# Order of the small float32 matmuls in a hybrid decoder's mixer: by array half instead of in turn

## The chip, the cores and the metric

The kernel runs on one core of one Trainium2 chip. The metric is the device time of one launch in microseconds. Before the change it is 1982.39 us, the median of three runs (1982.12 to 1985.22).

TensorE (PE in the profile) multiplies: a stationary operand (the weights, up to 128 rows by 128 columns) is loaded, a moving operand streams past it, and the result is written or added into PSUM, eight banks of 128 partitions by 512 float32. VectorE (DVE), ScalarE (ACT) and GpSimd (POOL) do the rest; SyncE (SP) issues most DMAs. A matmul whose operands have 64 rows uses the upper or the lower half of the array's rows, by the partitions on which they lie; one whose stationary operand has 64 columns uses the left or the right half of its columns, by the partitions to which it writes.

## The reference, cut to what matters

Two layers, each of them a SwiGLU half, a mixer and a second SwiGLU half, over 512 prompt tokens and 32 sample tokens (8 sequences of 4). The mixer has a sliding-window attention (8 query heads, 2 key/value heads of 64 dimensions, window 128, learned sinks) and a gated linear attention (GLA, 4 heads, key 64, value 128, chunks of 64 tokens):

```python
qg = q.reshape(B, N, Q, SWA_KV_HEADS, SWA_GROUP, HEAD_DIM)
s = jnp.einsum('bnqhgd,bnkhd->bnhgqk', qg, k) * (HEAD_DIM ** -0.5)
...
o = jnp.einsum('bnhgqk,bnkhd->bnqhgd', probs.astype(v.dtype), v)
```
```python
def step(S, inp):
    ...
    att = jnp.where(causal, jnp.einsum('bhid,bhjd->bhij', qb, kc * jnp.exp(-b)), 0.0)
    o = jnp.einsum('bhij,bhjv->bhiv', att, vc) + jnp.einsum('bhid,bhdv->bhiv', qb, S)
    S = jnp.exp(b_last[..., 0, :])[..., None] * S + jnp.einsum('bhjd,bhjv->bhdv', kc * jnp.exp(b_last - b), vc)
    return S, o
```

## The kernel before, in words

All activations stay in SBUF, feature-major: 8 tiles of 128 features by 544 tokens. The big products (projections and SwiGLU) take each weight as a high and a low part in fp32r and use three matmuls for each product (`product`, L769; `unit_product`, L809). They hold most of TensorE's time. The small products of the mixer are plain float32 and are what the change touches.

The order of each engine's work in a mixer is written out by hand: `mixer_steps()` makes one list `STEPS` that all engines walk through, and each engine does its share of every step. Steps named `in` are projection tiles; the small steps stand between them, so that VectorE and ScalarE work on one small step while TensorE does the next projection. Each engine's program is a fixed sequence, and it waits on semaphores.

The steps with small matmuls on TensorE that matter here:

- `score` (L1013), eight a layer, one for each pair of query block `b` (4) and head pair group `jj` (2). It computes four score tiles: `uu` is the head in the pair, `g` the key/value head. `g` picks partitions 0 to 63 or 64 to 127 of `qS` and `kS`, so the half of the array's rows, and writes to bank 4 + g. Block 0 has one key block (128 columns), the others have two (256 columns).
- `pv` (L1040), eight a layer: probabilities times values. `g` picks which 64 partitions of bank 6 are written, so the half of the array's columns; `kb` runs over one or two key blocks that are added up.
- `samp_s` (L1051, L1055), once a layer: scores of the sample tokens against the cache, for 8 sequences `b` and two row halves `g`, added up in PSUM over `b`.
- `kv` (L1126), eight steps a layer in four pairs: the state update of a GLA chunk. The chunk's half picks the rows, the head `hh` picks the columns, so there are four different quarters. An odd step does nothing here; the even one does both chunks and signals `kv_done` by 2.
- `att` (L1141) and `o` (L1155, L1163), four a layer: `o` adds, per head, one full matmul (values by masked scores, 128 rows) and for each of the two chunks a matmul of the state with the queries (64 rows, half picked by `hh`). In `o` 0 only one chunk has a state. The next step is `kv` or a projection.

`L975`, `L1185`, `L1191`, `L1203`, `L1216` and `L1229` are small products that the change leaves alone. VectorE's softmax of a unit starts with `score_done` (L2069), its copies of attention results with `pv_done` (L2178), the state update with `kv_done` (L2225, L2230), ScalarE's copy of the GLA output with `o_done` (L1635).

Of the kernel before, what the change touches and what calls it, by code (L numbers as in the profile page):

```python
# [24 lines left out]
P = 128  # L25
# [3 lines left out]
NB = 8  # L29
# [7 lines left out]
WIN = 128  # L37
HD = 64
PAST = 2048
EPS = 1e-6  # L40
CHUNK = 64
# [162 lines left out]
def trunk(nc, xT, stream, gains, lparams, wa2, cos_t, sin_t, swa_mask, samp_mask, gla_mask,  # L204
# [14 lines left out]
    with ctx:  # L219
# [18 lines left out]
        s_ring = sb("s_ring", [P, 4, 2, P], at=big)  # L238
# [38 lines left out]
        qG = mx("qG", [P, 2, T], 2 * U)  # L277
# [9 lines left out]
        kc = mx("kc", [P, NB, WIN], 13 * U)  # L287
        qz = mx("qz", [P, NB * (P + 16)], 15 * U)
# [473 lines left out]
        def _(pe):  # L762
# [183 lines left out]

            def product_order(b):

                return [(kb, g) for kb in range(0 if b else 1, 2) for g in range(2)]

            def mixer(l):
                ch = l * PL_LAYER + PL_MIX
                stage = l * 3 + 1
                for pos, (step, i) in enumerate(STEPS):
# [48 lines left out]
                    elif step == "score":  # L1003
# [5 lines left out]
                        o = 0 if b else WIN  # L1009
                        for uu in range(2):  # L1010
                            for g in range(2):
                                rows = slice(g * HD, (g + 1) * HD)
                                ins = pe.matmul(ps[:, 4 + g, uu * 256 + o:(uu + 1) * 256],  # L1013
                                                qS[rows, 2 * jj + uu, b * WIN:(b + 1) * WIN],
                                                kS[rows, k0:(b + 1) * WIN], start=True, stop=True)
# [18 lines left out]
                    elif step == "pv":  # L1034
                        b, jj = UNITS[i]
                        pe.wait_ge(m["pt_out"], i + 1)
                        for uu in range(2):
                            for kb, g in product_order(b):
                                o = (2 * g + uu) * 256 + kb * WIN
                                ins = pe.matmul(ps[g * HD:(g + 1) * HD, 6, uu * WIN:(uu + 1) * WIN],  # L1040
                                                vs_tok[:, b - 1 + kb, g * HD:(g + 1) * HD], p_t[:, o:o + WIN],
                                                start=kb == (0 if b else 1), stop=kb == 1, skip_group_check=True)
                        ins.then_inc(m["pv_done"], 1)
                    elif step == "samp_s":
                        pe.wait_ge(m["loaded"], 16 * N_LOADS)
                        pe.wait_ge(m["masked"], len(UNITS))
                        pe.wait_ge(m["q_set"], 1)
                        for b in range(NB):
                            for g in range(2):
                                rows = slice(g * HD, (g + 1) * HD)  # L1050
                                pe.matmul(ps[:, 4 + g, 0:WIN], qz[rows, b * P:(b + 1) * P], kc[rows, b, :],  # L1051
                                          start=b == 0, stop=b == NB - 1, skip_group_check=True)
                        for g in range(2):
                            rows = slice(g * HD, (g + 1) * HD)
                            ins = pe.matmul(ps[:, 4 + g, WIN:WIN + SAMP], qc[rows, :],  # L1055
                                            kS[rows, SEQ:T], start=True, stop=True)
# [60 lines left out]
                    elif step == "kv":  # L1117

                        if i % 2:
                            continue  # L1120
                        pe.wait_ge(m["att_out"], i // 2 + 1)
                        for h in range(GH):
                            pr, hh = divmod(h, 2)
                            for c in range(2):
                                rows = slice(c * CHUNK, (c + 1) * CHUNK)
                                ins = pe.matmul(ps[hh * HD:(hh + 1) * HD, 4 + c, pr * P:(pr + 1) * P],  # L1126
                                                klT[rows, i // 2, h * HD:(h + 1) * HD],
                                                v_tok[rows, i // 2, h * P:(h + 1) * P], start=True, stop=True)
                        ins.then_inc(m["kv_done"], 2)
                    elif step == "att":  # L1130
# [13 lines left out]
                    elif step == "o":  # L1144
# [8 lines left out]
                        for h in range(GH):  # L1153
                            pr, hh = divmod(h, 2)
                            pe.matmul(ps[:, 6 + hh, pr * P:(pr + 1) * P], v_tok[:, i, h * P:(h + 1) * P],  # L1155
                                      attm[:, i % 2, hh, pr, :], start=pr == 0, stop=False, skip_group_check=True)
                        for c in (2 * i, 2 * i + 1):
                            if c == 0:
                                continue
                            for pr in range(2):  # L1160
                                for hh in range(2):
                                    o = pr * P + (c % 2) * CHUNK
                                    ins = pe.matmul(ps[:, 6 + hh, o:o + CHUNK],  # L1163
                                                    s_ring[hh * HD:(hh + 1) * HD, c % 4, pr, :],
                                                    qG[hh * HD:(hh + 1) * HD, pr, c * CHUNK:(c + 1) * CHUNK],
                                                    start=False, stop=c == 2 * i + 1, skip_group_check=True)
                        ins.then_inc(m["o_done"], 1)
# [1306 lines left out]
```

## Time and profile before

| | us |
|---|---|
| median of 3 runs | 1982.39 |
| profiled execution, its own time | 1982.39 |
| span, first to last instruction | 1980.6 |
| TensorE busy | 1929.6 (97%) |
| VectorE busy | 1352.1 (68%) |
| ScalarE busy | 1103.3 (56%) |
| GpSimd busy | 1094.7 (55%) |

The two mixers lie at about 400 to 600 us and 1370 to 1575 us of the span. TensorE records come in two kinds: PE is the matmul, PEld the load of its stationary operand, which may overlap other matmuls. Matmuls overlap in their records, since the end of one is modelled with its way through the array, so what one costs in a stream is better read from the start of one group to the start of the next than from its duration. One float32 matmul of the program gives two PE records and two PEld records. In the forms, `64*128` is the stationary operand's rows and columns, and `64x256` the moving operand's partitions and columns.

### The profile page before, as it was taken

The numbers are of one execution on the slowest core, as the hardware profiler recorded it, in microseconds if no ns is written. First come the engines' busy times: TensorE is split into PE (matmuls) and PEld (weight loads), VectorE is DVE, ScalarE is ACT, GpSimd is POOL, SyncE is SP. The second block draws the span as 40 slices with busy tenths as digits, with TensorE's granted clock in tenths as the row PEclk, the third lists the DMA queues.
The fourth block names the chain that finished last, engine by engine and source line by source line (L and its number), as shares of the span: only waits on it lengthen the run. The fifth ranks groups of instructions, "written<-read, shape, count | busy, mean of one in ns | idle before, by whom it ended". The sixth has DMA issues, their size and how long they took to land.

```text
span 1980.6 us, 40845 instructions
## 1 busy us (share of the span) xinstructions
PE 1929.6 (97%) x15562; PEld 1899.0 (96%) x15562; DVE 1352.1 (68%) x2450; ACT 1103.3 (56%) x2184; POOL 1094.7 (55%) x811
## 2 busy tenths in 40 slices
PE   5999999999999999999999999999999999999997
PEld 5999999998989999999999999999888899999997
DVE  7976687487345986578678757865774458756774
ACT  4664566536234665566656646663552366645662
POOL 3675566732215566566766656675222166655663
PEclk9999999999989999999999999999998999999998
DMA  4233232421212233232323333224221222332331
GB/s 138 84 108 106 89 101 92 141 86 54 99 57 75 76 110 96 95 105 95 99 81 102 102 102 101 98 94 133 75 98 45 68 80 94 101 107 91 102 110 59
DMA packets 92114, 185.65 MB, mean 94 GB/s; under 512 B 12880, under 2 KB 22768, under 8 KB 91376
## 3 DMA queue, kind: packets, MB, share of 16 engines
q1 hardware_dynamic: 84096, 170.04, 26.2%
q10 hardware_dynamic: 7824, 13.00, 1.9%
q8 instruction: 124, 2.03, 0.4%
q14 instruction: 70, 0.57, 0.1%
HBM read 178.09 MB, written 6.95 MB: 93 GB/s over the span
## 4 chain that ended last, share of the span: by engine, by line
PE 90%; DVE 8%; issue 1%; ACT 1%; DMA 0%; POOLq 0%; POOL 0%; DVEq 0%; ACTq 0%
PE ps L809 56%; PE ps L769 21%; PE ps L818 7%; PE ps L1216 1%; PE ps L797 1%; PE ps L1229 1%; PE ps L1030 0%; PE ps L1040 0%; DVE t L2195 0%; DVE st L2074 0%; PE ps L1191 0%; DVE qS L2289 0%; PE ps L1013 0%; DVE h_end L1711 0%; PE ps L789 0%
## 5 line engine op out<-in xcount | busy, mean ns | idle before, releaser
L809 PE MATMUL ps<-rhs,w_hi 128*128 128x272 f32 x4256 | 805.0, 289 | 0.0
L809 PEld LDWEIGHTS ps<-rhs,w_hi 128*128 128x128 f32 x4256 | 669.7, 188 | 0.7 <-DVE ssum L1898 0.7
L809 PE MATMUL ps<-rhs,w_lo 128*128 128x272 f32 x2128 | 614.1, 289 | 0.0
L646 POOL TENSOR_TENSOR w_lo<-w_raw,w_hi 128x512 fp32r<-128x512 f32 x272 | 351.3, 1297 | 251.6 <-ACT w_hi L1316 251.6
L640 POOL TENSOR_TENSOR w_lo<-w_raw,w_hi 128x1024 fp32r<-128x1024 f32 x80 | 192.0, 2402 | 385.8 <-ACT w_hi L1260 371.1
L809 PEld LDWEIGHTS ps<-rhs,w_lo 128*128 128x128 f32 x2128 | 402.4, 189 | 0.0
L809 PE MATMUL ps<-act_c,w_hi 128*128 128x272 f32 x1792 | 354.5, 289 | 1.1 <-DVE h_mid L1749 0.8
L646 POOL TENSOR_TENSOR w_lo<-s_tmp,w_hi 128x512 fp32r<-128x512 f32 x216 | 282.9, 1321 | 32.9 <-ACT w_hi L1316 32.6
L809 PEld LDWEIGHTS ps<-act_c,w_hi 128*128 128x128 f32 x1792 | 287.7, 188 | 1.8 <-DVE h_mid L1749 1.2
L769 PE MATMUL ps<-h_mid,w_hi 128*128 128x272 f32 x1600 | 279.2, 293 | 0.0
L809 PE MATMUL ps<-act_c,w_lo 128*128 128x272 f32 x896 | 258.3, 288 | 0.0
L769 PEld LDWEIGHTS ps<-h_mid,w_hi 128*128 128x128 f32 x1600 | 230.0, 191 | 3.4 <-issue 2.8
L1316 ACT ACTIVATE w_hi<-ps 128x512 fp32r<-128x512 f32 x216 | 129.2, 598 | 182.1 <-DVE ps L1774 171.1
L1316 ACT ACTIVATE w_hi<-w_raw 128x512 fp32r<-128x512 f32 x272 | 172.0, 632 | 47.5 <-PE ps L809 40.3
L1316 ACT ACTIVATE w_hi<-s_tmp 128x512 fp32r<-128x512 f32 x216 | 136.7, 633 | 87.3 <-PE ps L809 85.9
L809 PEld LDWEIGHTS ps<-act_c,w_lo 128*128 128x128 f32 x896 | 169.3, 189 | 0.0
L769 PE MATMUL ps<-h_mid,w_lo 128*128 128x272 f32 x800 | 166.5, 290 | 0.0
L1774 DVE TENSOR_TENSOR s_tmp<-ps,w_raw 128x512 f32<-128x512 f32 x216 | 148.4, 687 | 17.2 <-POOL w_lo L646 3.1
L818 PE MATMUL ps<-act_p,pl_hi 128*128 128x272 f32 x768 | 159.4, 287 | 0.0
L1260 ACT ACTIVATE w_hi<-w_raw 128x1024 fp32r<-128x1024 f32 x76 | 80.1, 1057 | 129.9 <-PE ps L769 118.6
L1774 DVE TENSOR_TENSOR ps<-ps,w_raw 128x512 f32<-128x512 f32 x216 | 149.6, 692 | 2.8 <-ACT ps L1367 0.7
L1780 DVE TENSOR_TENSOR w_lo<-ps,w_hi 128x512 fp32r<-128x512 f32 x216 | 141.4, 684 | 1.2
(292 smaller groups left out, 3215.8 us busy)
## 6 DMA issues: line engine op xcount, KB each, us to landing
w_raw<-stream SPq DMA_DIRECT2D x380, 256.0 KB, 2.9
w_raw<-stream SPq DMA_DIRECT2D x80, 512.0 KB, 3.3
g_buf<-stream SPq DMA_DIRECT2D x52, 256.0 KB, 2.8
pl_raw<-stream SPq DMA_DIRECT2D x64, 192.0 KB, 2.8
x<-xT ACTq DMA_DIRECT2D x8, 272.0 KB, 5.9
y_d<-x SPq DMA_DIRECT2D x8, 272.0 KB, 2.1
s<-s_d ACTq DMA_DIRECT2D x2, 1024.0 KB, 5.3
s_s_d<-s ACTq DMA_DIRECT2D x2, 1024.0 KB, 3.9
```

What stands on the lines that cost most here:

```text
L640: pool.tensor_tensor(w_lo[:, p % RING, :], w_raw[:, p % RAW, :], w_hi[:, p % RING, :].bitcast(F32), ALU.subtract).then_inc(lo_ready, 1)
L646: pool.tensor_tensor(operand(w_lo, j, half), source(op, s, half), operand(w_hi, j, half).bitcast(F32), ALU.subtract).then_inc(pool_low, 1)
L769: ins = pe.matmul(dst[:, hf, :], w[:, slot, cols], r[:, hf * TH:(hf + 1) * TH], start=first and w is w_hi and r is rhs_hi, stop=last and r ...
L797: ins = pe.matmul(ps[:, 6 + at // TH, o:o + w], nrt[0:w, c:c + 1].to_broadcast([w, P]), ident[0:w, 0:w], start=True, stop=True)
L809: ins = pe.matmul(bank(s, at), w[:, k * P:(k + 1) * P], moving[:, k, side, r, :], start=fresh and k == 0 and w is hi and side == 0, stop=k ...
L818: ins = pe.matmul(bank(s, at), w[:, k * P:(k + 1) * P], act_p[:, k, side, hf * TH:(hf + 1) * TH], start=False, stop=k == PLAIN - 1 and sid ...
L1216: ins = pe.matmul(ps[0:w, 4, c:c + 1], sq_tile(h)[:, tb * P:tb * P + w], ones[:, 0:1], start=True, stop=True)
L1229: ins = pe.matmul(ps[:, 4 + 2 * (i % 2) + tb // 4, (tb % 4) * P:(tb % 4) * P + w], rt[0:w, c:c + 1].to_broadcast([w, P]), ident[0:w, 0:w], ...
L1260: act.activation(w_hi[:, p % RING, :], w_raw[:, p % RAW, :], ACT.Copy).then_inc(hi_ready, 1)
L1316: act.activation(operand(w_hi, j, half), source(op, s, half), ACT.Copy).then_inc(op_high, 1)
L1774: dve.tensor_tensor(source(name, s, half), first, second, ALU.add).then_inc(sum_made, 1)
L1780: dve.tensor_tensor(operand(w_lo, j, half), source(op, s, half), operand(w_hi, j, half).bitcast(F32), ALU.subtract).then_inc(dve_low, 1)
```

## The change

Five steps of TensorE's program are written in another order. The matmuls and their operands are the same.

- `score`: both `uu` of g = 0 first, then both of g = 1 (before: g = 0, g = 1 in turn).
- `pv`: all of g = 0, then all of g = 1 (before: in turn), by `a` from 0 to 3.
- `samp_s`: all eight sequences and the new tokens of g = 0, then of g = 1.
- `kv`: every step does its own chunk, with its own wait and its own signal of 1; before, the even step did both chunks in turn.
- `o`: head by head: the full matmul of a head, then its one or two state matmuls, then the next head. `start` is now set for each head, before only for the first of a bank.

```diff
-                        for uu in range(2):
-                            for g in range(2):
-                                rows = slice(g * HD, (g + 1) * HD)
+                        for g in range(2):
+
+                            rows = slice(g * HD, (g + 1) * HD)
+                            for uu in range(2):
                                 ins = pe.matmul(ps[:, 4 + g, uu * 256 + o:(uu + 1) * 256],
...
-                        for uu in range(2):
-                            for kb, g in product_order(b):
-                                o = (2 * g + uu) * 256 + kb * WIN
+                        for a in range(4):
+                            g, uu = divmod(a, 2)
+                            for kb in range(0 if b else 1, 2):
+                                o = a * 256 + kb * WIN
                                 ins = pe.matmul(ps[g * HD:(g + 1) * HD, 6, uu * WIN:(uu + 1) * WIN],
                                                 vs_tok[:, b - 1 + kb, g * HD:(g + 1) * HD], p_t[:, o:o + WIN],
...
-                        for b in range(NB):
-                            for g in range(2):
-                                rows = slice(g * HD, (g + 1) * HD)
-                                pe.matmul(ps[:, 4 + g, 0:WIN], qz[rows, b * P:(b + 1) * P], kc[rows, b, :],
-                                          start=b == 0, stop=b == NB - 1, skip_group_check=True)
                         for g in range(2):
                             rows = slice(g * HD, (g + 1) * HD)
+                            for b in range(NB):
+                                pe.matmul(ps[:, 4 + g, 0:WIN], qz[rows, b * P:(b + 1) * P], kc[rows, b, :],
+                                          start=b == 0, stop=b == NB - 1)
...
-                        if i % 2:
-                            continue
                         pe.wait_ge(m["att_out"], i // 2 + 1)
+                        rows = slice((i % 2) * CHUNK, (i % 2 + 1) * CHUNK)
                         for h in range(GH):
                             pr, hh = divmod(h, 2)
-                            for c in range(2):
-                                rows = slice(c * CHUNK, (c + 1) * CHUNK)
-                                ins = pe.matmul(ps[hh * HD:(hh + 1) * HD, 4 + c, pr * P:(pr + 1) * P],
...
-                        ins.then_inc(m["kv_done"], 2)
+                            ins = pe.matmul(ps[hh * HD:(hh + 1) * HD, 4 + i % 2, pr * P:(pr + 1) * P],
...
+                        ins.then_inc(m["kv_done"], 1)
...
                         for h in range(GH):
                             pr, hh = divmod(h, 2)
-                            pe.matmul(ps[:, 6 + hh, pr * P:(pr + 1) * P], v_tok[:, i, h * P:(h + 1) * P],
-                                      attm[:, i % 2, hh, pr, :], start=pr == 0, stop=False, skip_group_check=True)
-                        for c in (2 * i, 2 * i + 1):
-                            if c == 0:
-                                continue
-                            for pr in range(2):
-                                for hh in range(2):
-                                    o = pr * P + (c % 2) * CHUNK
+                            at, bank = pr * P, 6 + hh
+                            pe.matmul(ps[:, bank, at:at + P], v_tok[:, i, h * P:(h + 1) * P],
+                                      attm[:, i % 2, hh, pr, :], start=True, stop=False)
+                            for c in (2 * i, 2 * i + 1):
+                                if c == 0:
+                                    continue
+                                o = at + (c % 2) * CHUNK
```

TensorE's program around the second `o` of a layer (step `o` 1, after `att` 2 and before `kv` 4), before the change. L1155 and L1163 are the full matmuls and the state matmuls; in the changed file they are L1149 and L1155:

```order
L1141 MATMUL ps<-qG,kG 128x128 x4
L1155 MATMUL ps<-attm,v_tok 128x128 x4
L1163 MATMUL ps<-qG,s_ring 128x64 x8
L1126 MATMUL ps<-v_tok,klT 64x128 x8
L943 MATMUL ps<-g_buf,ones 128x272 x2
```

and of the changed kernel:

```order
L1134 MATMUL ps<-qG,kG 128x128 x4
L1149 MATMUL ps<-attm,v_tok 128x128
L1155 MATMUL ps<-qG,s_ring 128x64 x2
L1149 MATMUL ps<-attm,v_tok 128x128
L1155 MATMUL ps<-qG,s_ring 128x64 x2
L1149 MATMUL ps<-attm,v_tok 128x128
L1155 MATMUL ps<-qG,s_ring 128x64 x2
L1149 MATMUL ps<-attm,v_tok 128x128
L1155 MATMUL ps<-qG,s_ring 128x64 x2
L1119 MATMUL ps<-v_tok,klT 64x128 x8
```

The four full matmuls, which stood together, now stand each ahead of its own head's two state matmuls.

TensorE's program at the first pair of `kv` steps, with the waits, before:

```order
L1141 MATMUL ps<-qG,kG 128x128 [waits m_ga_out]
L1141 MATMUL ps<-qG,kG 128x128 x3
L1126 MATMUL ps<-v_tok,klT 64x128 [waits m_att_out]
L1126 MATMUL ps<-v_tok,klT 64x128 x7
L769 MATMUL ps<-h_mid,w_hi 128x272 [waits lo_ready,m_in_used]
```

and of the changed kernel:

```order
L1134 MATMUL ps<-qG,kG 128x128 [waits m_ga_out]
L1134 MATMUL ps<-qG,kG 128x128 x3
L1119 MATMUL ps<-v_tok,klT 64x128 [waits m_att_out]
L1119 MATMUL ps<-v_tok,klT 64x128 x3
L1119 MATMUL ps<-v_tok,klT 64x128 [waits m_att_out]
L1119 MATMUL ps<-v_tok,klT 64x128 x3
L769 MATMUL ps<-h_mid,w_hi 128x272 [waits lo_ready,m_in_used]
```

The eight matmuls are split in two groups of four, one for each row half, with a wait ahead of each. In `score`, `pv` and `samp_s` the rows of the program look the same before and after, since the matmuls of both halves have the same names and shapes; what moves there is what the diff shows.

## Rows read from the trace of the kernel before

**Rows 1.** The profile's page, sections 1 and 4.
```profile
PE 1929.6 (97%) x15562; PEld 1899.0 (96%) x15562; DVE 1352.1 (68%) x2450; ACT 1103.3 (56%) x2184; POOL 1094.7 (55%) x811
...
PE 90%; DVE 8%; issue 1%; ACT 1%; DMA 0%; POOLq 0%; POOL 0%; DVEq 0%; ACTq 0%
```

**Rows 2.** Waits of TensorE, 410 to 610 us: waited for, us, times, longest.
```profile
PE ps L769 <- DVE mixS_lo L2093: 2.4, 2, 1.6
...
PE ps L1030 <- DVE qS L2178: 1.1, 2, 0.8
...
PE ps L1110 <- DVE vG L2132: 0.5, 1, 0.5
```

**Rows 3.** Busy time by window, L1013 alone: window, length, busy (xinstructions), clock, DMA.
```profile
433.39:433.45 0.06, 0.05 (x2) 0.05 (x2) 1.00 0.00 0
433.45:433.71 0.26, 0.26 (x2) 0.25 (x4) 1.00 0.00 0
```

**Rows 4.** Timeline, two narrow windows: start, us, engine, line, op, tiles, count.
```profile
433.73 0.59 PE L1013 MATMUL ps<-kS,qS 64*128 64x256 f32 x3
...
434.15 0.38 PE L1013 MATMUL ps<-kS,qS 64*128 64x256 f32 x2
```

**Rows 5.** Busy time by window, L975 alone, then L1203 alone.
```profile
444.90:445.10 0.20, 0.19 (x1) 0.19 (x2) 1.00 0.00 0
...
552.30:552.37 0.07, 0.06 (x8) 0.07 (x10) 1.00 0.63 234
```

**Rows 6.** Timeline of TensorE, pv, score and the transposes after them, 432.8 us.
```profile
432.81 0.66 PE L1040 MATMUL ps<-a_buf,vs_tok 128*64 128x128 f32 x8
433.40 1.14 PE L1013 MATMUL ps<-kS,qS 64*128 64x256 f32 x8
434.46 1.09 PE L1030 MATMUL ps<-ident,sq_buf 128*128 128x128 f32 x8
```

**Rows 7.** Timeline of TensorE, a later pv and short score, and samp_s.
```profile
452.23 1.09 PE L1040 MATMUL ps<-a_buf,vs_tok 128*64 128x128 f32 x16
453.25 0.72 PE L1013 MATMUL ps<-kS,qS 64*128 64x128 f32 x8
453.94 1.06 PE L1030 MATMUL ps<-ident,sq_buf 128*128 128x128 f32 x8
...
494.74 2.06 PE L1051 MATMUL ps<-kc,qz 64*128 64x128 f32 x32
496.63 0.31 PE L1055 MATMUL ps<-kS,qc 64*128 64x32 f32 x4
```

**Rows 8.** Timeline of TensorE, steps o and kv.
```profile
539.80 0.66 PE L1163 MATMUL ps<-qG,s_ring 64*128 64x64 f32 x8
540.39 0.67 PE L1126 MATMUL ps<-v_tok,klT 64*64 64x128 f32 x16
...
547.84 1.16 PE L1155 MATMUL ps<-attm,v_tok 128*128 128x128 f32 x8
548.93 1.11 PE L1163 MATMUL ps<-qG,s_ring 64*128 64x64 f32 x16
549.97 0.67 PE L1126 MATMUL ps<-v_tok,klT 64*64 64x128 f32 x16
550.56 1.18 PE L943 MATMUL ps<-g_buf,ones 128*128 128x272 f32 x4
...
568.60 1.05 PE L1155 MATMUL ps<-attm,v_tok 128*128 128x128 f32 x8
569.58 1.11 PE L1163 MATMUL ps<-qG,s_ring 64*128 64x64 f32 x16
```

**Rows 9.** Busy time by window, all engines, and the granted clock (PEclk).
```profile
530.40:533.70 3.30, 3.30 (x15) 3.30 (x16) 1.03 (x3) 0.00 (x0) 0.58 (x1) 0.50 0.02 5
547.00:552.00 5.00, 4.75 (x55) 3.61 (x53) 2.67 (x7) 2.96 (x4) 2.35 (x1) 1.00 0.04 8
578.40:588.20 9.80, 9.80 (x47) 9.74 (x47) 0.31 (x3) 0.41 (x2) 0.00 (x0) 0.50 0.45 174
```

More of the change, by code:

```diff
@@ L945, in square_sum @@
                 return ins
-            def product_order(b):
-                return [(kb, g) for kb in range(0 if b else 1, 2) for g in range(2)]
             def mixer(l):
@@ L1036, in mixer @@
                         pe.wait_ge(m["pt_out"], i + 1)
-                        for uu in range(2):
-                            for kb, g in product_order(b):
-                                o = (2 * g + uu) * 256 + kb * WIN
+                        for a in range(4):
+                            g, uu = divmod(a, 2)
+                            for kb in range(0 if b else 1, 2):
+                                o = a * 256 + kb * WIN
                                 ins = pe.matmul(ps[g * HD:(g + 1) * HD, 6, uu * WIN:(uu + 1) * WIN],
                                                 vs_tok[:, b - 1 + kb, g * HD:(g + 1) * HD], p_t[:, o:o + WIN],
-                                                start=kb == (0 if b else 1), stop=kb == 1, skip_group_check=True)
+                                                start=kb == (0 if b else 1), stop=kb == 1)
                         ins.then_inc(m["pv_done"], 1)
@@ L1117, in mixer @@
                     elif step == "kv":
-                        if i % 2:
-                            continue
                         pe.wait_ge(m["att_out"], i // 2 + 1)
+                        rows = slice((i % 2) * CHUNK, (i % 2 + 1) * CHUNK)
                         for h in range(GH):
                             pr, hh = divmod(h, 2)
-                            for c in range(2):
-                                rows = slice(c * CHUNK, (c + 1) * CHUNK)
-                                ins = pe.matmul(ps[hh * HD:(hh + 1) * HD, 4 + c, pr * P:(pr + 1) * P],
-                                                klT[rows, i // 2, h * HD:(h + 1) * HD],
-                                                v_tok[rows, i // 2, h * P:(h + 1) * P], start=True, stop=True)
-                        ins.then_inc(m["kv_done"], 2)
+                            ins = pe.matmul(ps[hh * HD:(hh + 1) * HD, 4 + i % 2, pr * P:(pr + 1) * P],
+                                            klT[rows, i // 2, h * HD:(h + 1) * HD],
+                                            v_tok[rows, i // 2, h * P:(h + 1) * P], start=True, stop=True)
+                        ins.then_inc(m["kv_done"], 1)
                     elif step == "att":
@@ L1154, in mixer @@
                             pr, hh = divmod(h, 2)
-                            pe.matmul(ps[:, 6 + hh, pr * P:(pr + 1) * P], v_tok[:, i, h * P:(h + 1) * P],
-                                      attm[:, i % 2, hh, pr, :], start=pr == 0, stop=False, skip_group_check=True)
-                        for c in (2 * i, 2 * i + 1):
-                            if c == 0:
-                                continue
-                            for pr in range(2):
-                                for hh in range(2):
-                                    o = pr * P + (c % 2) * CHUNK
[L1163 to L1166, printed above, removed]
+                            at, bank = pr * P, 6 + hh
[5 more added lines that the diff above has]
+                                o = at + (c % 2) * CHUNK
+                                ins = pe.matmul(ps[:, bank, o:o + CHUNK],
+                                                s_ring[hh * HD:(hh + 1) * HD, c % 4, pr, :],
+                                                qG[hh * HD:(hh + 1) * HD, pr, c * CHUNK:(c + 1) * CHUNK],
+                                                start=False, stop=c == 2 * i + 1)
                         ins.then_inc(m["o_done"], 1)
```

## The prediction, made before the changed kernel ran

> **What bounds the kernel now.** I read the page first. TensorE is busy for 1929.6 of 1980.6 us, and it has 90% of the chain that ended last [rows 1]. So a microsecond added to TensorE's own work costs a microsecond, unless TensorE would otherwise wait there for somebody. The waits are few: between 410 and 610 us, one layer's mixer, TensorE waits 2.4 us for DVE's mixS_lo, 1.1 us for its qS and 0.5 us for its vG [rows 2]. The second layer's mixer is built alike. The edit touches five steps of the mixer on TensorE, twice (two layers): eight `score`, eight `pv`, one `samp_s`, four pairs of `kv`, four `o` per layer. No operand, shape or DMA changes; only the order of the matmuls, and `kv` has two waits and two signals where it had one.
>
> **What small matmuls do side by side.** These are float32 matmuls, and each shows as two records: four score matmuls are x8, sixteen of L1203 x32. I call a record a pass. In narrow windows one sees how many run at once: L1013 (64 rows, g = 0 and g = 1 in turn) has 2 in its first 60 ns, and up to 433.71 still 2, with 4 weight loads: the two next passes have their weights and wait [rows 3]. They start at 433.73, 0.33 after the first two, and from there to the last two at 434.15 two rounds take 0.42, 0.21 each [rows 4]. L975, both matmuls on the same 16 rows, has 1; L1203, which goes over eight different places of the array, has 8 in its first 60 ns [rows 5]. So passes on different parts of the array (row halves, column halves, quarters) run together, passes on the same part one after another, and the blocked second pass of one matmul does not hold back the first pass of the next matmul on another part. The order before always puts different parts next to each other; the order after puts all work of one half first. The question is how far the array looks past a blocked pass.
>
> The Trainium skill, TensorE: Matmul & The Clock Gate, Part 3, says that only weight loads are pulled ahead when the row group differs, and that matmuls start and end in program order. The trace disagrees: by that rule the second pass of a matmul would stand in front of the next matmul, and there could not be 8 under way within 60 ns. With that rule the order before would already be nearly serial, and the sum below would shrink to its `o` term.
>
> **What the rows of before give as unit costs.** I measure a group from its start to the start of the next group.
> - Full score (256 columns): 433.40 to 434.46, 1.06 us for 4 rounds of two passes [rows 6]; the first round is 0.10 longer than the others [rows 4], which I read as a first weight load that nothing hides. Short score (128 columns): 0.69 us [rows 7].
> - pv: 0.59 us for 4 rounds [rows 6], 1.02 for 8 [rows 7]: 0.43 for 4 more, 0.109 a round.
> - samp_s: 1.89 us for 16 rounds [rows 7], at most 0.118 a round; I take the 0.112 of L1163 below, which has the same weights.
> - kv: four passes at once, 0.59 us for 4 rounds [rows 8].
> - o: L1155, 128 rows, 8 passes one after another, 1.09 us when it comes from 64-row matmuls (547.84) and 0.98 when it comes from 128-row ones (568.60); L1163, 64 rows, 0.59 us for 4 rounds, 1.04 for 8, so 0.112 a round [rows 8]. What stands over the rounds (0.59 - 3 x 0.112 = 0.25 instead of 0.11) is the price of coming from and going to another split of the array.
>
> **o, step by step.** After the edit each head does its one 128-row matmul, then its one or two 64-row matmuls on one half, then the next head's 128-row one: eight changes of split where there were two, and the 64-row passes no longer have a partner, whatever the array looks past, since the 128-row matmul between needs all of it. Per head with two chunks: 128-row part 1.09 - 6 x 0.112 = 0.42, 64-row part 4 passes alone = the 4 rounds' 0.59; 1.01. Four heads 4.04 against 1.09 + 1.04 = 2.13: +1.9 us, three times a layer. In o 0 only one chunk: 0.42 + 0.59 - 2 x 0.112 = 0.79, four times 3.15, against 1.09 + 0.59 = 1.68: +1.5 us. Per layer 7.2 us. The low end: were the changes of split free once they repeat, 6 passes of 0.112 per head are 2.7 against 2.13, so +0.6, and +0.1 for o 0: 1.8 per layer.
>
> **score, pv, samp_s, kv.** No row shows a queue of several blocked passes on one part. From below the cost is 0 (the array finds the other half's work however far back). Below nothing it cannot go: no pass is dropped, and two halves are all there is. From above it is fully serial: score +0.85 and +0.45 (4 rounds), pv +0.87 and +0.44, samp_s +1.8, kv +1.3 a pair; 19 us a layer. I take the value nearest to rows 3: a part holds one running pass and one waiting with its weights loaded, and the third one blocks everything behind it. Then the second half starts when the first half's last but one pass is done, with its first weight load in the open (0.10 us; 0.05 for pv's 64 columns):
> - full score: 2 rounds later, 2 x 0.213 + 0.10 = 0.53, six times; short 2 x 0.112 + 0.10 = 0.32, twice: 3.8
> - pv: 8 passes a half, 6 x 0.109 + 0.05 = 0.70, six times; block 0 with 4 passes 0.27, twice: 4.7
> - samp_s: 16 passes a half, 14 x 0.112 + 0.10 = 1.7
> - kv: column halves still alternate, row halves do not: 2 x 0.109 + 0.04 = 0.26, four times: 1.0. The added wait is on the semaphore value that the first half had already seen; behind it stand the second half and the next projection, nobody waits for it longer than for kv itself.
>
> With o that is 18.4 us per layer.
>
> **What waits absorb.** In the attention stage TensorE's waits for qS and vG (1.1 + 0.5) come after a score or pv that the longer work fills: 1.6 back. The score itself starts DVE's softmax, so its own delay is passed on, not absorbed. The 2.4 us for mixS_lo stand right behind o 2, whose +1.9 and kv's +0.3 go into them, except what comes back since DVE's s_ring waits for kv: I take 1.8 back. Nothing else: the weight pipeline follows TensorE, and the waits before L1203 and L1216 are themselves started by TensorE. Net 18.4 - 3.4 = 15.0 per layer, 30 in all. The profiled execution took 1982.39 us, its span 1980.6; it is the median itself. So 1982.4 + 30 = 2012.
>
> **Rivals.**
> 1. The array looks far back. Then score, pv, samp_s and kv keep their pairs (their queue is 8 to 32 passes) and only o costs: 7.2 - 1.8 = 5.4 per layer, 1993 us. For it: it does pass blocked work in rows 5; against: nothing is seen to pass more than one blocked pass on a part, and rows 3 show exactly one further load per part. The skill's page named above gives TensorE a 64-deep reorder window for loads; if matmuls followed them, even samp_s would fit in nearly whole, and this rival is what comes out. No row here shows that depth.
> 2. More than the forecast: fully serial, 26 - 3.4 = 23 per layer, 2028 us; or the granted clock falls in the thinned o. It was 0.50 (1.2 GHz) at 530.4 to 533.7, and 1.00 (2.4 GHz) in 547 to 552 with o 1, kv and a wait in it; in the low stretches TensorE gets through fewer than 5 passes a microsecond, in the other through 11 [rows 9]. A grouped o lasts 4 us with much of the array idle, so up to some 2 us for each o that is followed by a fall.
> 3. No change: changes of split free when repeated and far look-back: 1.8 per layer, all absorbed: 1982 to 1986.
> 4. Faster: the low-clock stretches go. One lasts 9.8 us at 0.50, the other at least 3.3 [rows 9]; half of each is lost, 6.5 us per layer if both vanish, 13 in all. Against rival 1's +11 that is 1980 us at best, a little faster; on top of rival 3 it is 1971. It decides from the point where more comes back than o costs. Against it: what runs ahead of these stretches is gs_o and gss, which the change does not touch, and a longer o makes TensorE sparser, not denser.
>
> **Chances.** Forecast 0.66 (its own range 2004 to 2020, from the slot rule being off by half a round each way and absorption by 3), rival 1 0.20, rival 2 0.07, no change 0.04, faster 0.03. About 0.2%, 4 us, can be told from no change. So faster 0.03, same 0.04, slower 0.93. From 1991 to 2020 the range takes in rival 1 and the forecast.
>
> **What would show it.** In the profile after: o of two chunks about 4.0 us instead of 2.1, rows of L1149 and L1155 in turn; the start of a full score to the next group 1.6 us instead of 1.06, pv of 8 matmuls 1.7 instead of 1.02, samp_s 3.6 instead of 1.9. If score and pv stay at their old lengths and o grows, rival 1 holds. If o grows by under 1 us, the price of a change of split is wrong. If TensorE's groups grow as said and the total does not, the waits took more than I allowed.

## The result, and the profile after

| | before | after |
|---|---|---|
| median | 1983.81 us (4 runs, 1982.12 to 1985.9) | 2001.94 us (4 runs, 2000.6 to 2005.46) |
| span of the profiled execution | 1980.6 us | 1998.2 us |
| TensorE busy | 1929.6 us | 1951.4 us |
| its share of the chain that ended last | 90% | 93% |

The change makes the kernel slower: ratio 1.0094, 95% interval 1.0076 to 1.0111. Forecast was 2012, so +30; measured is +18. The sign and the `o` term were right. The terms of `score`, `pv` and `kv` were too large.

First the timeline of TensorE in the changed kernel at a `pv` with 4 matmuls and one with 8, each with the score that follows (columns: start, us, engine, line, op, tiles, form, count). The same groups of before are in [rows 6, 7].

```profile
434.13 0.67 PE L1038 MATMUL ps<-a_buf,vs_tok 128*64 128x128 f32 x8
434.73 1.14 PE L1010 MATMUL ps<-kS,qS 64*128 64x256 f32 x8
...
442.85 1.58 PE L1038 MATMUL ps<-a_buf,vs_tok 128*64 128x128 f32 x16
444.36 1.14 PE L1010 MATMUL ps<-kS,qS 64*128 64x256 f32 x8
445.43 0.66 PE L1027 MATMUL ps<-ident,g_buf 128*128 128x128 f32 x4
...
455.30 0.72 PE L1010 MATMUL ps<-kS,qS 64*128 64x128 f32 x8
455.98 0.41 PE L1027 MATMUL ps<-ident,sq_buf 128*128 128x128 f32 x2
```

The full score takes 444.36 to 445.43, 1.07 us, as before (1.06); the short one 0.68 (before 0.69). The `pv` with 4 matmuls takes 0.60 us, as before, and the one with 8 takes 1.51 us instead of 1.02. So here grouping by half costs nothing while a half has 4 passes, and costs when it has 8. `samp_s`, with 16 passes a half and 2 more for the new tokens:

```profile
498.12 2.16 PE L1049 MATMUL ps<-kc,qz 64*128 64x128 f32 x18
500.00 0.30 PE L1051 MATMUL ps<-kS,qc 64*128 64x32 f32 x2
500.11 1.72 PE L1049 MATMUL ps<-kc,qz 64*128 64x128 f32 x14
501.68 0.30 PE L1051 MATMUL ps<-kS,qc 64*128 64x32 f32 x2
501.91 0.39 PE L769 MATMUL ps<-h_mid,w_hi 128*128 128x272 f32 x1
```

From 498.12 to 501.91 it takes 3.79 us; before it was 494.74 to the end of the new tokens' passes (L1055), 2.13 us. The first half has 16 passes of L1049 and then 2 of L1051. When L1051 begins, at 500.00, L1049 has 18 passes behind it (x18): the first half's 16 and only 2 of the second half. The number of `samp_s` records in narrow windows agrees: it goes from 2 to 4 between 499.76 and 499.78, 1.65 us after the start, which is 0.10 for the first weight load and 14 rounds of 0.11. So the second half started 14 passes late, and most of it (x14) runs alone.

Then `o` 1, the one that [rows 8] show as 547.84 to 549.97, and the `kv` behind it:

```profile
554.85 0.49 PE L1149 MATMUL ps<-attm,v_tok 128*128 128x128 f32 x2
555.26 0.66 PE L1155 MATMUL ps<-qG,s_ring 64*128 64x64 f32 x4
555.85 0.49 PE L1149 MATMUL ps<-attm,v_tok 128*128 128x128 f32 x2
...
558.27 0.66 PE L1155 MATMUL ps<-qG,s_ring 64*128 64x64 f32 x4
558.86 0.68 PE L1119 MATMUL ps<-v_tok,klT 64*64 64x128 f32 x16
559.47 0.72 PE L943 MATMUL ps<-g_buf,ones 128*128 128x272 f32 x2
```

Each head takes 0.42 us for the 128-row matmul and 0.59 for its two 64-row ones; four heads are 558.86 - 554.85 = 4.01 us instead of 2.13. `kv`, split in two row halves with a wait between, takes 0.61 us instead of 0.59.

TensorE's waits in the first mixer (waited for, us, times, longest), to be set beside [rows 2], and one of the second mixer:

```profile
PE ps L1038 <- ACT a_buf L1541: 1.2, 1, 1.2
...
PE ps L1027 <- DVE qS L2170: 0.4, 1, 0.4
...
PE ps L769 <- DVE mixS_lo L2085: 1.0, 1, 1.0
```

In the first mixer the 2.4 us for mixS_lo and the 0.5 us for vG are gone. The wait for qS fell from 1.1 to 0.4, but the one of `pv` for the copied probabilities (a_buf) is 1.2 us, where it was 0.4 before. In the second mixer all is the same, except that 1.0 of the 2.4 us for mixS_lo (the last row) is left. Why the two differ is told below, with the granted clock.

Per layer, TensorE's groups grew by: `o` 3 x 1.88 + 1.44 = 7.1 us (`o` 0: four heads of 0.78 are 3.12 instead of 1.68), `pv` 6 x 0.49 = 2.9, `samp_s` 1.66, `score` and `kv` 0.1 together. That is 11.8 us, 23.5 in both layers, against 17.6 us of span. Some 4.8 us went into TensorE's waits (2.9 in the first mixer, 1.9 in the second), and the rest is within the scatter of one execution.

### The profile page after: what moved, and what is told of

Read it like the earlier page. It is cut to its first block, busy times and chain, and to the rows that moved or that the text cites. A ratio compares the mean times of both kernels' runs of the same rounds, so it can differ in the third digit from the quotient of the medians.

```text
span 1998.2 us, 40845 instructions
## 1 busy us (share of the span) xinstructions
PE 1951.4 (98%) x15562; PEld 1916.9 (96%) x15562; DVE 1350.1 (68%) x2450; ACT 1102.8 (55%) x2184; POOL 1094.3 (55%) x811
## 4 chain that ended last, share of the span: by engine, by line
PE 93%; DVE 5%; issue 1%; ACT 1%; DMA 0%; POOLq 0%; POOL 0%; DVEq 0%; ACTq 0%
PE ps L809 56%; PE ps L769 23%; PE ps L818 7%; PE ps L1038 1%; PE ps L1155 1%; PE ps L1027 1%; PE ps L1149 1%; PE ps L797 1%; PE ps L1208 1%; PE ps L1221 1%; PE ps L1010 0%; PE ps L1183 0%; DVE h_end L1703 0%; DVE h_end L1700 0%; PE ps L789 0%
```

## The experiments

Three theories stood after the result. **Q3**: each part of the array (a half or a quarter) holds one running pass and three waiting ones; the fifth pass for the same part blocks everything behind it. **Q1**: the forecast's rule, one waiting pass. **W**: one window over all parts together.

### The parts of the change alone

e1 puts only `o` in the changed order, e2 only `pv` and `samp_s`, e3 only `score` and `kv`; each hunk does what its part of the change's diff does, and the rest is the kernel before.

> Only step o is written head by head; score, pv, samp_s and kv stay as before. By the order costs read off the trace of before, an o with two chunks takes 4.01 us (before 2.13) and o 0 takes 3.12 (before 1.68), 7.1 us per layer, less what TensorE's wait for mixS_lo (2.4 us in a layer) takes in. Theory (changes of split and lost partners, and both halves of that alone): slower by 14.2 less 2 to 5 us, so 9 to 12 us, about 0.5%. Rival (the loss of the full change comes mainly from the attention steps): under 5 us.

Measured: 1993.43 us against 1981.91, ratio 1.0055 (1.0041 to 1.0069), so +11 us. TensorE's wait for mixS_lo fell from 2.4 to 1.1 us in the first mixer. As expected.

> Only pv and samp_s are grouped by half. Theory Q3 (a part of the array holds one running pass and three waiting ones; the fifth pass for it blocks everything behind): pv with 8 matmuls 1.51 us (before 1.02), pv with 4 matmuls 0.59 as before, samp_s with its last two matmuls 3.79 (before 2.13): 4.6 us per layer, 9.2 in all, less 1 to 3 us of waits for vG and qS: slower by 6 to 8 us, 0.3 to 0.4%. Rival Q1 (one waiting pass, the forecast's rule): pv 1.72 and 0.86 us, 12 us raw, slower by 9 to 11. Rival (waits of TensorE swallow it, since vector work sets the pace of the attention stage): within 2 us.

Measured: 1991.3 us, ratio 1.0041 (1.0027 to 1.0055), +8 us, at the upper end of what Q3 gives and below Q1's 9 to 11. `pv` with 8 matmuls takes 1.51 us and `samp_s` 3.79, as Q3 says. The waits of its first mixer:

```profile
PE ps L769 <- DVE mixS_lo L2092: 2.4, 2, 1.6
...
PE ps L1041 <- ACT a_buf L1548: 1.2, 1, 1.2
...
PE ps L1030 <- DVE qS L2177: 0.4, 1, 0.4
```

The wait for a_buf is 1.2 us here too, and the one for mixS_lo is whole. So the grown wait comes with `pv` and `samp_s`, not with `o`, `score` or `kv` (e3, below, has it at 0.4 us), and it eats most of what the waits for qS and vG give back. The traces show where it arises. In the changed kernel, two rows stand side by side (start, us), GpSimd's and the vector engine's:

```profile
469.37 2.39 POOL L640 TENSOR_TENSOR w_lo<-w_raw,w_hi 128x1024 fp32r<-128x1024 f32 x1 [11.93 <-ACT w_hi L1252]
469.59 2.19 DVE L2067 TENSOR_TENSOR st<-st,nsk 128x4 f32<-128x4 f32 x1
```

The vector engine's step is a tiny one of the softmax that these probabilities need. It took 0.16 us before and takes 2.19 here, and it ends 0.02 us after GpSimd's operation. Before, the softmax was through at 467.40 and GpSimd's operation began at 467.51; the vector operation that then fell beside it, the scan (L2195), took 3.38 us, where it takes 1.29 in the changed kernel, and it is no part of this softmax. The vector engine waits longer for the `pv` ahead of this softmax (0.79 us ahead of its copy, 0.31 before), and the softmax starts (L2061, L2069 before) 2.30 us ahead of GpSimd's operation instead of 2.98. So a slip of 0.7 us puts its last steps beside that operation, 2 us are lost there, and TensorE's wait grows by 0.7 to 0.8. The second mixer and the profiles of e2 and e6 show the same pair, those of e1 and e3 the order of before; no run moved GpSimd's operation by itself, so this is read from the coincidence and not tested.

> Only score and kv are grouped by row half, kv with a wait and a signal for each half. Theory Q3: score has 4 passes a half, which all fit in the queue of their half, so 1.07 and 0.65 us as before; kv 0.61 as before: within 1 us of before. Rival Q1: full score 1.60, kv 0.86: 4.8 us per layer, slower by 6 to 9 us. Rival W (the array looks past three blocked passes in all, whichever part they are for): score as before, but kv, whose second half stands behind six blocked passes of two column halves, would take 0.8 us or more, +0.2 us eight times, +2 us at most.

Measured: 1982.56 us, ratio 1.0003 (0.9994 to 1.0012): nothing. Full scores take 1.07 us and short ones 0.68. Q1 is out with this run alone. The three ratios add up to 1.0099, the full change gave 1.0094.

### How deep the queue is, and what o pays for

e4 was run once, for its trace. It does all the work, in orders chosen to tell the queue's depth and to take `o`'s two costs apart. `pv` goes in runs of (half, chunk), `samp_s` in runs of 2 matmuls a half in layer 0 and 4 in layer 1; `o` does all full matmuls and then the state matmuls by half in layer 0, and two heads at a time in layer 1:

```diff
+                        runs = [(g, uu) for uu in range(2) for g in range(2)] if l == 0 else \
+                            [(0, 0), (1, 0), (1, 1), (0, 1)]
...
+                        run = 2 if l == 0 else 4
+                        for b0 in range(0, NB, run):
                             for g in range(2):
                                 rows = slice(g * HD, (g + 1) * HD)
...
+                                for b in range(b0, min(b0 + run, NB)):
...
```

The hunk of `o` is left out here.

> Probes of the queue's depth, read in the trace; all work is done, only its order differs. Q3: a run of r passes for one half delays the other half by r - 4 rounds and costs no more in later runs. samp_s, layer 0 in runs of 2 matmuls (4 passes) per half: 1.89 us, as in turn; layer 1 in runs of 4 matmuls (8 passes): 4 rounds of 0.112 more, 2.34 us. pv with 8 matmuls, layer 0 in runs of 4 passes (half 0, 1, 0, 1): 1.02 us; layer 1 as 4, 8, 4 passes (half 0, 1, 1, 0): 1.02 us too. o: layer 0 all full matmuls first as before, then the state matmuls by half (8 passes each): L1163's group 4 rounds longer, 1.04 + 0.45 = 1.49 us, the full part unchanged at 1.09: the lost partners without changes of split. Layer 1 pair of heads by pair of heads, state matmuls of a pair in turn: two changes of split more, partners kept: 2.47 us instead of 2.13. Rival Q1: samp_s 2.1 and 2.6 us, pv 1.2 or more. Rival W (window of all parts together): samp_s layer 0 as in turn, pv 4, 8, 4 slower than 1.1, since half 0's last passes stand behind four or more blocked ones.

The timeline of e4: `samp_s` of layer 0, `o` 1 of layer 0, `pv` of layer 1, `o` 1 of layer 1.

```profile
496.15 2.16 PE L1055 MATMUL ps<-kc,qz 64*128 64x128 f32 x32
498.04 0.41 PE L1059 MATMUL ps<-kS,qc 64*128 64x32 f32 x4
...
549.45 1.16 PE L1160 MATMUL ps<-attm,v_tok 128*128 128x128 f32 x8
550.54 1.60 PE L1168 MATMUL ps<-qG,s_ring 64*128 64x64 f32 x16
552.07 0.34 PE L1130 MATMUL ps<-v_tok,klT 64*64 64x128 f32 x4
...
1414.49 1.16 PE L1042 MATMUL ps<-a_buf,vs_tok 128*64 128x128 f32 x16
1415.58 0.49 PE L1013 MATMUL ps<-kS,qS 64*128 64x256 f32 x2
...
1522.22 0.71 PE L1176 MATMUL ps<-attm,v_tok 128*128 128x128 f32 x4
1522.86 0.66 PE L1183 MATMUL ps<-qG,s_ring 64*128 64x64 f32 x8
1523.45 0.71 PE L1176 MATMUL ps<-attm,v_tok 128*128 128x128 f32 x4
1524.09 0.66 PE L1183 MATMUL ps<-qG,s_ring 64*128 64x64 f32 x8
1524.68 0.56 PE L1130 MATMUL ps<-v_tok,klT 64*64 64x128 f32 x12
```

- `samp_s` in runs of 4 passes a half: 1.89 us, exactly as in turn. Q1's 2.1 is refuted. `pv` of layer 0, also in runs of 4 passes a half, takes 1.07 to 1.08 us, 0.05 more than in turn; what that is was not tried.
- `o`, full matmuls first and then 8 passes for each half: 1.09 us for L1160, unchanged, and 1.53 for L1168 (1.04 in turn, 1.49 expected). So the lost partners alone cost 0.5 us, without one more change of split.
- `o`, two heads at a time with partners kept: 1522.22 to 1524.68, 2.46 us (2.47 expected, 2.13 before): two more changes of split cost 0.33 us, 0.17 each. The changed kernel has six more than before, 6 x 0.17 = 1.0, and twice the 64-row rounds, 8 x 0.112 = 0.9; together the 1.9 us measured.
- `pv` 4, 8, 4: 1.09 us against 1.02 expected and 1.02 in turn. It is a little slower, not faster, and W and Q3 do not part here as the expectation said, since both let the late passes in when the second half's fifth pass starts.
- `samp_s` of layer 1 in runs of 8 passes took 2.89 us with the new tokens (1467.94 to 1470.83), against 2.13 in turn, so +0.76, where +0.45 was expected. By Q3 a later run of 8 comes in just as its half falls empty, so its first weight load may stand in the open each time; that would be 0.1 us for each, as an estimate from the first round in [rows 4]. It fits the 0.3 us in excess, and the 0.07 of `pv`, but it was not tested.

e8, run once for its trace, asks W and Q3 again, with `kv` quarter by quarter and two more run lengths in `samp_s`:

```diff
-                        for h in range(GH):
-                            pr, hh = divmod(h, 2)
-                            for c in range(2):
...
+                        for c in range(2):
+                            rows = slice(c * CHUNK, (c + 1) * CHUNK)
+                            for hh in range(2):
+                                for pr in range(2):
+                                    h = 2 * pr + hh
...
```

> kv in runs of one quarter of the array: 4 passes for each of the four quarters, one quarter after the other. Q3 (each part has its own queue of three waiting passes): the fourth quarter starts within 0.05 us of the first although 9 unfinished passes of three other quarters stand ahead of it, and kv takes 0.61 to 0.65 us. Rival W (one window over all parts, of a little more than the six blocked passes that the changed kernel's kv goes past): the fourth quarter starts at least one round later, kv 0.7 us or more. samp_s, layer 0 in runs of 3 matmuls (6 passes): the first pass of the second half starts with the third pass of the first half (2 rounds, 0.33 us, after the start). Layer 1 in runs of 6 matmuls (12 passes): it starts with the ninth pass, 1.0 us after the start. Rival (a fixed time or a fixed share of the run): both start at the same place.

Busy time by window, of `kv`'s line alone (window, length, PE busy and count, PEld busy and count, clock, DMA), and then of `samp_s`'s line in layer 0 and in layer 1:

```profile
550.26:550.33 0.07, 0.06 (x4) 0.06 (x5) 1.00 0.00 0
550.33:550.38 0.05, 0.05 (x4) 0.05 (x8) 1.00 0.00 0
...
494.67:494.88 0.21, 0.20 (x1) 0.20 (x2) 1.00 0.00 0
494.90:494.98 0.08, 0.08 (x2) 0.08 (x2) 1.00 0.00 0
495.01:495.03 0.02, 0.02 (x4) 0.02 (x3) 1.00 0.00 0
...
1465.51:1465.70 0.19, 0.18 (x1) 0.19 (x2) 1.00 0.00 0
1466.38:1466.50 0.12, 0.12 (x3) 0.12 (x2) 1.00 0.00 0
1466.53:1466.60 0.07, 0.07 (x4) 0.07 (x3) 1.00 2.32 293
```

Within 0.07 us of its start `kv` has 4 passes under way, one in each quarter. In program order 12 passes stand before the fourth of these, 3 of them running and 9 waiting. The weights of the four next passes follow (x8 loads). It took 0.62 us. A window over all parts as small as the one that the changed kernel's `pv` would need (3 waiting passes) would have stopped at the second quarter. `samp_s` of layer 0 starts at 494.68; up to 494.98 only passes of the first half have begun (x1, and x2 where the record of the first still lasts when the second begins), and at 495.01 there are four records, two of them new: the third pass of the first half and the first of the second, 0.33 us after the start. In layer 1, which starts at 1465.52, the same happens with the ninth pass: the row from 1466.53 on has four records, and in narrower windows they are there from 1466.51, 0.99 us after the start. Runs of 6 and 12 passes start the other half 2 and 8 passes late: run length less 4, both times. W (of that size) and a fixed delay are out.

### Fewer changes of split than before

If a change of split costs 0.17 us, the kernel before has some to give. e5 puts the state matmuls of `o` right behind `att` (both 64-row), then `kv`, then the full matmuls ahead of the next projection; it groups the sums of squares by shape, and turns one broadcast round:

```diff
+                    if step == "o" and STEPS[pos + 1][0] != "kv":
+                        pe_steps.append((pos, "of", i))
+                    elif step == "kv" and i % 2 and STEPS[pos - 2][0] == "o":
+                        pe_steps.append((pos, "of", STEPS[pos - 2][1]))
...
-                        for h in range(GH):
-                            for tb in range(5):
+                        for h, tb in [(h, tb) for h in range(GH) for tb in range(4)] + [(h, 4) for h in range(GH)]:
```

> All orders in turn as before, and fewer changes of split: in o the 64-row state matmuls come first (right behind att, which is 64-row too), then kv, then the 128-row matmuls right ahead of the next projection; in the sums of squares (L1216 before) the four heads' 128-column matmuls first and then the four 32-column ones; the second broadcast (L1229 before) starts with its 32-row piece. Each change of split taken out should give 0.09 to 0.19 us: two for each of three o (6 x 2 x 0.17 = 2.1 us in both layers), about 0.2 us three times in the sums of squares, twice that where the clock is low (1 to 2 us in all), 0.3 us for the broadcasts: 3 to 5 us faster, 0.15 to 0.25%. Rival: kv, now right behind the state matmuls, waits for the vector engine's mask of att (0.8 us of work, 1.0 us of cover), which would eat the gain of o: faster by under 1.5 us.

Measured: 1982.76 us against 1982.32, ratio 1.0003 (0.9995 to 1.0012). One of its waits says why:

```profile
PE ps L1133 <- DVE attm L2252: 3.1, 3, 1.6
```

`kv` (L1133) waits 3.1 us for the vector engine's mask, 0.9 before. The full matmuls had been the cover of that latency. The rival was right.

e7 keeps `kv` behind the full matmuls (`att`, state, full, `kv`) and all else of e5:

```diff
+                    if step == "o":
+                        pe_steps.append((pos, "of", i))
```

> As e5, but kv stays behind the full matmuls of o: att, state matmuls, full matmuls, kv. Only the change of split between att and o is saved (6 times 0.15 to 0.2 us), with the sums of squares and the broadcast as in e5. The vector engine's mask of att has the cover it had before, so the waits of 0.5 and 1.6 us that e5 showed before kv should be gone. Theory: faster than before by 2 to 3 us (0.10 to 0.15%), at the edge of what five rounds can tell. Rival: the run-to-run scatter, which comes with the low-clock stretches, hides it: ratio within 0.9992 to 1.0008.

Measured: 1979.65 us (12 runs) against 1982.61 (16 runs), ratio 0.9990 (0.9980 to 0.9999): 2 us faster than the kernel before, just clear of noise. `o` 1 with the `att` before it and the `kv` behind it, and the wait:

```profile
548.52 0.71 PE L1146 MATMUL ps<-qG,kG 64*128 64x128 f32 x8
549.07 1.01 PE L1164 MATMUL ps<-qG,s_ring 64*128 64x64 f32 x16
550.00 1.16 PE L1171 MATMUL ps<-attm,v_tok 128*128 128x128 f32 x8
551.09 0.67 PE L1131 MATMUL ps<-v_tok,klT 64*64 64x128 f32 x16
551.69 1.18 PE L943 MATMUL ps<-g_buf,ones 128*128 128x272 f32 x4
...
PE ps L1131 <- DVE attm L2250: 0.9, 1, 0.9
```

State and full matmuls take 549.07 to 551.09, 2.02 us, where before they took 2.13, and `att` takes 0.55 where before it took 0.65 (547.19 to 547.84). From `att` to the end of `kv` that is 3.17 us instead of 3.37, so one change of split less gave 0.20 here. (The step from the state matmuls' 64*128 weights to `kv`'s 64*64 must count as a change for this: both orders have two changes between 64 and 128 rows up to `kv`.) `o` 0 and `o` 2 show the same 0.20, so 1.2 of the 2 us come from `o`; the sums of squares and the broadcast were not taken apart. The wait before `kv`, 3.1 us in e5, is 0.9 again. This version beats both kernels.

### The full change once more

> The changed kernel once more, on the chip of these comparisons, to set it beside the parts. If the parts add up (o 11.0 us, pv and samp_s 8.1, score and kv 0.6, by their ratios), it is slower by 19 to 20 us, ratio 1.0095 to 1.0100; if waits are shared between the parts, so that one part's delay fills what another part would have filled too, it is more than the sum, over 1.0105; if one part's delay gives cover to another's, less than 1.0090.

Measured: 2000.2 us against 1982.32, ratio 1.0092 (1.0078 to 1.0105). It is a little below the sum of its parts (1.0099), and the intervals do not tell them apart. So the parts add up within what can be measured; whether they share waits stays open.

## Why the prediction was right, point by point

The measured 2001.94 us lies in the stated range of 1991 to 2020, but 2 us below the forecast's own 2004 to 2020. It is in the range because that takes in rival 1. The `o` term was right in mechanism and size; the mechanism taken for `score`, `pv`, `samp_s` and `kv` was not.

- **TensorE is the bound, so its own work counts in full, less the waits.** Right: 23.5 us more of it, less 4.8 us of waits, gave 17.6 us of span in the profiled execution.
- **`o` head by head: +1.9 us with two chunks, +1.5 for `o` 0, 7.2 per layer.** Right: 1.88, 1.44 and 7.1. e1 shows it alone, +11 us, and e4 that both halves of the argument are real, 1.0 us from changes of split and 0.9 from lost partners.
- **One running and one waiting pass, the third blocks.** This is the step that failed. A part takes three waiting passes. The two next weight loads in [rows 3] showed that the next pass had its weights; they were read as the whole queue, and they are only its front. So `score` 3.8 us a layer was 0.05, `kv` 1.0 was 0.1 and `pv` 4.7 was 2.9 (the second half starts with the fifth pass, 4 rounds late, not 6, and the short `pv` fits whole). `samp_s` 1.7 was 1.66: with 18 passes a half, new tokens included, the second half starts 14 late by Q3. The sum had 14 too, from 16 passes less 2, so it is right by luck: by its own rule, with all 18 passes, it should have been 16.
- **Waits absorb 3.4 us a layer.** Too much: 2.9 in the first mixer, 1.9 in the second. For the attention stage 1.6 had been taken, and 0.5 came back, since a wait of 0.4 us grew to 1.2, which the forecast had not seen. For mixS_lo 1.8 had been taken. Where the clock stays full, 1.4 of the 2.4 us came back (second mixer here, first mixer of e6); where it fell behind `o` 2, all of the 2.4.
- **Rival 1, the array looks far back (1993 us).** Wrong too, but right for `score` and `kv`; the measured 2001.94 lies between it and the forecast. By Q3 in place of Q1 the forecast's own sum is 7.2 + 2.9 + 1.7 + 0.1 = 11.9 per layer, less 3.4, 17 in all: 1999 us. With the waits as measured, 1.9 to 2.9, it is 2000 to 2002 us.
- **Granted clock.** In rival 2 the clock falls in the thinned `o`; in rival 4 the low stretches go. The second did not come, the first did in part. The windows below are of the changed kernel, the fourth in its second mixer, and then of the kernel before (busy time of TensorE, its loads and the other engines; third from the end the granted clock, 1.00 being 2.4 GHz):

```profile
400.00:660.00 260.00, 254.26 (x2058) 238.61 (x2057) 148.68 (x259) 110.81 (x212) 80.65 (x38) 0.97 0.21 71
554.00:559.50 5.50, 5.50 (x52) 4.31 (x50) 1.50 (x3) 1.59 (x3) 2.35 (x1) 1.00 0.08 25
572.50:575.70 3.20, 3.20 (x28) 2.80 (x27) 2.63 (x8) 1.24 (x4) 0.00 (x0) 0.57 0.49 164
1551.63:1554.80 3.17, 2.39 (x29) 2.00 (x28) 2.83 (x7) 1.49 (x4) 0.00 (x0) 1.00 0.45 165
```

```profile
400.00:640.00 240.00, 231.43 (x1966) 217.80 (x1964) 144.00 (x250) 104.95 (x204) 77.83 (x36) 0.96 0.21 72
561.90:565.00 3.10, 2.29 (x29) 1.89 (x28) 2.97 (x5) 1.20 (x3) 1.17 (x1) 1.00 0.26 69
```

The clock is full in `o` 1. Behind `o` 2 it falls to near half rate at 572.5 to 575.7; at the same place of the program before, 561.9 to 565.0, it was full. But in the second mixer of the same profile it stays full there (1551.63 to 1554.80). In e6, the same kernel, it is the other way round: 1.00 in the first mixer, 0.64 in the second (1552.84 to 1556.00). In e1 it falls in the second mixer, already in the last head of `o` 2 (0.51 from 1544.43 to 1551.10). Each of these three falls goes with a wait for mixS_lo that is gone: the slower projection fills it. So in the changed kernel the fall costs only 0.2 to 0.3 us (from `kv` to `o` 3 5.33 and 5.41 us with it, 5.11 and 5.10 without); in e1, where it begins earlier, it costs 1.7 us. Whether the grouped `o` brings these falls is not shown: they come in three of six mixers with it, and in neither of the two in the profile before. The means over the first mixer hardly differ, 0.97 after and 0.96 before, and over the whole execution it is 0.988 both times. So the clock carries no measurable part of the 18 us.

## What to carry to other kernels

Small matmuls on different parts of the array run side by side if no part gets more than four passes (two float32 matmuls) ahead of the others; so order by part in short runs, not strictly in turn. A 128-row matmul between 64-row ones costs twice, about 0.17 us for each change of split (how many rows and columns of the array a matmul takes) and the partner of every pass around it, so group by split first. And before a group is moved, ask which latency it covers: in e5 the moved group was the cover of a wait, and the gain was gone.

## What the runs showed of the hardware

- Of each part of the array one pass runs and three wait; passes of other parts go past them, past 9 waiting ones in e8's `kv`. In the changed kernel's `pv` the second half started with the fifth pass of the first, 0.48 us after the start. All matmuls here are float32, so four passes are also two matmuls, and eight instructions with the weight loads; which of these is counted is not shown.
- The Trainium skill, TensorE: Matmul & The Clock Gate, Part 3, has matmuls start in program order; here they do not. The first table of that page of the Trainium skill gives TensorE a queue of 64 with partial reorder. What these runs show is a limit for each part, and it is reached after four passes.
- A change between 128-row and 64-row matmuls costs 0.17 us in a stream of float32 passes (e4), also when it repeats at once; one change less gave 0.20 us (e7).
- While GpSimd's 2.39-us operation on 128x1024 elements ran, a vector operation on 128x4 elements took 2.19 us instead of 0.16 (e2, e6 and the changed kernel).
- The same kernel, before, ran from 1979.2 to 1986.8 us on these chips. This scatter is larger than any of the effects in e3, e5 and e7, so none of those can be read from one execution.
